# A hybrid decoder step on one core: the first stage's products put in the order in which their loads land, one gate tile's load issued ahead of a wait, and one block-diagonal product for the sample rows of a mixture window

## The reference, cut to what matters

```
mod = silu(c) @ w_ada + b_ada                      # six vectors per conditioning row: shift, scale, gate, twice
h = rms_norm(x, norm_mix_w) * (1 + sc1) + sh1
dn_qkv, dn_z, dn_a, dn_b, ssm_xbc, ssm_z, ssm_dt, gate_dn, gate_ssm = split(h @ w_in)
q, k, v = silu(causal_conv(dn_qkv, dn_conv_buf)); o, dn_state = gated_delta(q, k, v, g(dn_a), beta(dn_b))
x_, B, C = silu(causal_conv(ssm_xbc, ssm_conv_buf)); y, ssm_state = ssd(x_, dt(ssm_dt), B, C)
merged = sigmoid(gate_dn) * (o @ w_dn_out) + sigmoid(gate_ssm) * (y @ w_ssm_out)
x = x + gt1 * (merged @ w_out)
h = rms_norm(x, norm_ffn_w) * (1 + sc2) + sh2
x = x + gt2 * moe(h)                               # 4 groups x 8 experts, top-1 group, top-2 experts, SwiGLU, MOE_FF = 256
y = rms_norm(x, final_norm_w) * (1 + scale) + shift
```

## Time and profile before

| | |
|---|---|
| median of 3 executions | 838.47 us (837.27 to 840.47) |
| the profiled execution | 839.85 us |
| its span, first to last instruction | 838.1 us |
| mean granted TensorE clock | 0.942 |
| PE busy | 728.8 us, 87% of the span |
| chain that ended last: PE | 81% |
| DVE, ACT, POOL busy | 264.0, 195.1, 97.5 us |
| DMA | 195.88 MB, mean 234 GB/s |

### The profile page before, as it was taken

One profiled execution on the slowest core, in us unless ns is written; L12 is line 12 of the kernel. 1 busy time (PEld: TensorE's weight loads), 2 busy tenths in 40 slices (PEclk: granted clock), 3 DMA queues, 4 the chain that ended last, 5 costly groups with the idle time before them and its releaser, 6 DMA issues.

```text
span 838.1 us, 19950 instructions
## 1 busy us (share of the span) xinstructions
PE 728.8 (87%) x8393; PEld 529.4 (63%) x8394; DVE 264.0 (32%) x737; ACT 195.1 (23%) x500; POOL 97.5 (12%) x229
## 2 busy tenths in 40 slices
PE   2779999999988975998988999973998989999985
PEld 1567777787766654776766777733655656656554
DVE  0145412430134350666683112144111111111122
ACT  1221113112731322122223200051111112121225
POOL 7000000001011222100000000001212221222200
PEclk9869999999999996999998999985899999999996
DMA  7835579999444954651002706875899999999901
GB/s 264 228 103 201 201 245 327 327 327 334 121 112 122 260 148 103 200 179 26 1 2 74 266 0 268 334 300 204 313 413 411 414 413 411 415 412 414 385 15 56
DMA packets 108728, 195.88 MB, mean 234 GB/s; under 512 B 9964, under 2 KB 71097, under 8 KB 100488
## 3 DMA queue, kind: packets, MB, share of 16 engines
q1 hardware_dynamic: 106760, 189.94, 63.1%
q0 software_dynamic: 1920, 5.25, 1.7%
HBM read 185.40 MB, written 9.77 MB: 233 GB/s over the span
## 4 chain that ended last, share of the span: by engine, by line
PE 81%; DVE 6%; DMA 4%; issue 4%; ACT 3%; SPq 1%; POOL 0%; ACTq 0%; DVEq 0%; POOLq 0%
PE ps L1142 17%; PE ps L533 10%; PE ps L1212 7%; PE ps L506 5%; PE ps L546 5%; PE ps L430 4%; PE ps L451 4%; PE ps L1084 4%; PE ps L509 3%; PE ps L434 2%; PE ps L496 2%; DMA arena<-in_w_ada 1%; SPq L811 1%; PE ps L540 1%; DVE arena L1894 1%
## 5 line engine op out<-in xcount | busy, mean ns | idle before, releaser
L1142 PE MATMUL ps<-arena 128*128 128x288 f32 x576 | 144.8, 411 | 0.0
L1142 PEld LDWEIGHTS ps<-arena 128*128 128x128 f32 x576 | 109.3, 192 | 31.2 <-issue 1.0
L533 PE MATMUL ps<-arena 128*32 128x128 f32 x2432 | 86.7, 278 | 15.3 <-issue 12.8
L533 PEld LDWEIGHTS ps<-arena 128*32 128x32 f32 x2432 | 69.3, 111 | 39.4 <-issue 38.2
L1212 PE MATMUL ps<-arena 128*128 128x288 f32 x256 | 76.2, 427 | 14.2 <-DMA arena<-in_w_in 10.3
L1212 PEld LDWEIGHTS ps<-arena 128*128 128x128 f32 x256 | 45.3, 194 | 30.1 <-DMA arena<-in_w_in 10.6
L506 PE MATMUL ps<-level,arena 32*128 32x256 f32 x624 | 44.8, 401 | 0.5 <-DVE arena L775 0.5
L546 PE MATMUL ps<-arena,hact 128*32 128x256 f32 x608 | 40.7, 385 | 0.0
L770 DVE TENSOR_TENSOR h_row<-h_row,ps 128x64 f32<-128x64 f32 x38 | 8.4, 221 | 96.6 <-ACT h_row L628 96.6
L404 POOL DMA_INDIRECT arena<-h_rows,idx_now x38 | 37.6, 988 | 9.5 <-issue 9.5
L1084 PE MATMUL ps<-arena,cT 128*32 128x128 f32 x1024 | 33.8, 292 | 4.6 <-DMA arena<-in_w_ada 4.6
(11 more groups left out here) (432 smaller groups left out, 983.0 us busy)
## 6 DMA issues: line engine op xcount, KB each, us to landing
arena<-in_w_exp_gate SPq DMA_DIRECT2D x32, 1024.0 KB
arena<-in_w_exp_up SPq DMA_DIRECT2D x32, 1024.0 KB
arena<-in_w_exp_down SPq DMA_DIRECT2D x32, 1024.0 KB
arena<-in_w_ada SPq DMA_DIRECT2D x12, 2048.0 KB, 10.2
arena<-in_w_in SPq DMA_DIRECT2D x18, 1024.0 KB, 5.9
arena<-in_w_ada_final SPq DMA_DIRECT2D x4, 2048.0 KB, 14.9
arena<-in_w_in SPq DMA_DIRECT2D x16, 512.0 KB, 4.7
arena<-in_state_ssm_rec SPq DMA_DIRECT2D x8, 512.0 KB, 6.0
```

The source lines that it names most:

```text
L533: l = mm(ps[CW * q:CW * (q + 1), 5, 0:P].rearrange("p (g f) -> p g f", g=2), xwin[:, at:at + CW], gate_up[:, :, k, f:f + HF], start=(k == ...
L1142: l = mm(ps[:, 2 + 2 * sl + m, 0:TOK], w_ring[sl][:, k, m * P:(m + 1) * P], HN[:, k, :], start=(k == 0), stop=(k == KT - 1))
```

## The change

In the first stage PE's stream is rewritten: the w_ada tiles one and two no longer stand behind the tables; x's transposes, the tables' transposes, tile three, the sum of squares and tile four follow. `busy(n, bank)` multiplies the identity by itself n times into a bank that is not read. DVE makes HN's product with the inverse root ahead of the fourth w_ada tile's copy, and shares the scale and shift with ACT (four of eight row tiles each). The 24 small columns are made with `wsm` as the stationary operand (8 products of 288 columns, a result of 24 rows), in `project(0)` between its two w_in tiles with the first halo's transposes; `small_rows` turns them to token rows after the second. On SP the first two w_in tiles are issued ahead of the small loads, and gate 7's load behind the first half's four stores instead of behind the wait for them and gates 8 to 11.

In the windows, PT gets 384 columns: 256 for the prompt and 4 times 32 for the samples. `iota` is -1 in those of the 128 sample columns that don't belong to a partition's own group of 32, so that PT is block-diagonal there, and one product of 128 by 128 replaces the four of 32 by 32.

```diff
+        PTW = SEQ + 4 * SMP
+        PT, iota = late[:, 0:PTW], late[:, PTW:2 * PTW]
...
-            link(g.iota(iota, pattern=[[1, TOK]], base=0, channel_multiplier=0, allow_small_or_imprecise_dtypes=True))
+            link(g.iota(iota[:, 0:SEQ], pattern=[[1, SEQ]], base=0, channel_multiplier=0, allow_small_or_imprecise_dtypes=True))
+            own = iota[:, SEQ:PTW].rearrange("p (m t) -> p m t", t=SMP)
+            link(g.iota(own, pattern=[[0, 4], [1, SMP]], base=SEQ, channel_multiplier=0, allow_small_or_imprecise_dtypes=True))
+            for step, base in ((-SMP, 0), (SMP, SMP - 1)):
+                link(g.affine_select(out=own, in_=own, pattern=[[step, 4], [0, SMP]], base=base,
+                                     channel_multiplier=1 if step < 0 else -1, compare_op=ALU.is_ge, fill=-1.0))
...
-                for m in range(4):
-                    r = slice(CW * m, CW * (m + 1))
-                    l = mm(ps[r, 4, 0:2 * P], PT[r, SEQ:TOK], y_row[r, :], start=False, stop=last)
+                l = mm(ps[:, 4, 0:2 * P], PT[:, SEQ:PTW], y_row[:, :], start=False, stop=last)
...
-                ts(PT, iota[:, 0:TOK], slot_tab[:, 0, bass.ds(c, 1)], slot_tab[:, 1, bass.ds(c, 1)], ALU.is_equal,
+                ts(PT, iota, slot_tab[:, 0, bass.ds(c, 1)], slot_tab[:, 1, bass.ds(c, 1)], ALU.is_equal,
                    ALU.mult).then_inc(S("pt"), 1)
...
+            for sl in range(2):
+                load(w_ring[sl], wi[:, :, sl * WN:(sl + 1) * WN], f"win_ld{sl}")
             load(wsm[:, :, 0:4], wi[:, :, C_A:C_A + 4], "small_ld")
...
-            for sl in range(2):
-                load(w_ring[sl], wi[:, :, sl * WN:(sl + 1) * WN], f"win_ld{sl}")
...
+            e.wait_ge(S("gate_mm"), 5)
+            gate_load(6)
             for g in range(2):
-                e.wait_ge(S("gate_mm"), 5 + g)
-                gate_load(6 + g)
                 for j in range(4):
                     e.wait_ge(S("hs_new"), 4 * g + j + 1)
                     e.dma_start(hs_out[(4 * g + j) * P:(4 * g + j + 1) * P], Hs_g[g][:, j]).then_inc(S("hs_stored"), 16)
+                if g == 0:
+                    e.wait_ge(S("gate_mm"), 6)
+                    gate_load(7)
...
-            e.wait_ge(S("tab_ld"), 16 * 10)
-            tr(ps[:, 0, 0:A_ROWS], tabA, ident[0:A_ROWS, 0:A_ROWS])
-            tr(ps[:, 0, 128:128 + B_ROWS], tabB, ident[0:B_ROWS, 0:B_ROWS]).then_inc(S("first_mm"), 1)
-
...
+            def busy(n, bank):
+                for _ in range(n):
+                    mm(ps[:, bank, 0:P], ident[:, :], ident[:, :], start=True, stop=True)
             e.wait_ge(S("cT"), 1)
-            for i in range(2):
-                for sl in range(2):
-                    e.wait_ge(S(f"ada_ld{sl}"), i * 16 + 16)
-                    if i:
-                        e.wait_ge(S("mod_read"), sl + 1)
-                    ada_products(sl, 6 + sl)
-                    e.wait_ge(S("mod_row"), 2 * i + sl + 1)
-                    ada_transposed(sl, 6 + sl)
-                if i == 0:
-                    e.wait_ge(S("x_ld"), 48)
-                    for k in range(KT):
-                        if k >= 4:
-                            e.wait_ge(S("xT"), k - 3)
-                        for t, (o, p) in enumerate(TILES):
-                            l = tr(ps[:, k % 4 + 2, o:o + p], x_tok[0:p, t, k * P:(k + 1) * P], ident[0:p, 0:p])
-                        l.then_inc(S("x_mm"), 1)
+            busy(8, 0)
+            def first_block(i):
+                sl = i % 2
+                e.wait_ge(S(f"ada_ld{sl}"), i // 2 * 16 + 16)
+                if i >= 2:
+                    e.wait_ge(S("mod_read"), i - 1)
+                ada_products(sl, 6 + sl)
+                e.wait_ge(S("mod_row"), i + 1)
+                ada_transposed(sl, 6 + sl)
+            first_block(0)
+            busy(3, 0)
+            first_block(1)
+            busy(3, 0)
+            e.wait_ge(S("x_ld"), 48)
+            for k in range(KT):
+                if k >= 4:
+                    e.wait_ge(S("xT"), k - 3)
+                for t, (o, p) in enumerate(TILES):
+                    l = tr(ps[:, k % 4 + 2, o:o + p], x_tok[0:p, t, k * P:(k + 1) * P], ident[0:p, 0:p])
+                l.then_inc(S("x_mm"), 1)
+            e.wait_ge(S("tab_ld"), 16 * 10)
+            tr(ps[:, 1, 0:A_ROWS], tabA, ident[0:A_ROWS, 0:A_ROWS])
+            tr(ps[:, 1, 128:128 + B_ROWS], tabB, ident[0:B_ROWS, 0:B_ROWS]).then_inc(S("first_mm"), 1)
+            first_block(2)
             e.wait_ge(S("sq"), 1)
-            e.wait_ge(S("col"), 1)
             for k in range(KT):
                 l = mm(ps[:, 0, 0:TOK], ones[:, :], sq[:, k, :], start=(k == 0), stop=(k == KT - 1))
             l.then_inc(S("ms_mm"), 1)
-            e.wait_ge(S("small_ld"), 16 * 14)
-            e.wait_ge(S("xT"), 8)
-            for i, halo in enumerate((dn_halo, ssm_halo)):
+            first_block(3)
+            def small_products():
+                e.wait_ge(S("small_ld"), 16 * 14)
+                for k in range(KT):
+                    l = mm(ps[0:24, 0, 0:TOK], wsm[:, k, :], HN[:, k, :], start=(k == 0), stop=(k == KT - 1))
+                l.then_inc(S("gsm_mm"), 1)
                 for m in range(NQ):
-                    l = tr(ps[:, 2 + i, m * 24:(m + 1) * 24], halo[:, m * P:(m + 1) * P], ident[0:24, 0:24])
+                    l = tr(ps[:, 1, m * 24:(m + 1) * 24], dn_halo[:, m * P:(m + 1) * P], ident[0:24, 0:24])
                 l.then_inc(S("halo_mm"), 1)
 
+            def small_rows():
+                e.wait_ge(S("gsm_row"), 1)
+                for m in range(NQ):
+                    l = tr(ps[:, 0, m * 24:(m + 1) * 24], ssm_halo[:, m * P:(m + 1) * P], ident[0:24, 0:24])
+                l.then_inc(S("halo_mm"), 1)
+                e.wait_ge(S("halo_read"), 1)
+                for t, (o, p) in enumerate(TILES):
+                    l = four(t, ps[:, 1, t * 24:(t + 1) * 24], gsm_rows[:, o:o + p], ident[0:24, 0:24])
+                l.then_inc(S("gsm_mm"), 1)
+            e.wait_ge(S("root"), 1)
+            busy(10, 0)
             e.wait_ge(S("hn"), 1)
             e.wait_ge(S("x_mod"), KT)
-            for t, (o, p) in enumerate(TILES):
-                for k in range(KT):
-                    l = four(t, ps[:, 1, t * 24:(t + 1) * 24], HN[:, k, o:o + p], wsm[:, k, :], start=(k == 0), stop=(k == KT - 1))
-            l.then_inc(S("gsm_mm"), 1)
-            e.wait_ge(S("halo_read"), 2)
-            e.wait_ge(S("mod_read"), 4)
...
+                    if first:
+                        (small_rows if sl else small_products)()
...
-                for k in range(KT):
+                for k in range(KT // 2 if n == 1 else KT):
...
+                if i == 2:
+                    e.wait_ge(S("first_mm"), 2)
+                    v.tensor_copy(colB[:], ps[:, 1, 128:128 + B_ROWS])
+                    link(v.tensor_copy(colA[:], ps[:, 1, 0:A_ROWS]))
+                if i == 3:
+                    e.wait_ge(S("root"), 1)
+                    for k in range(KT):
+                        l = tt(HN[:, k, :], xT[:, k, :], rstd[:], ALU.mult)
+                    link(l)
...
-            e.wait_ge(S("root"), 1)
-            modulated(HN)
+            e.nop().then_inc(S("x_scaled"), KT)
+            for k in range(KT // 2, KT):
+                ts(HN[:, k, 0:SEQ], HN[:, k, 0:SEQ], scl[:, k, 0:1], modT[:, SHIFT1 + k, 0:1], ALU.mult, ALU.add).then_inc(S("x_mod"), 1)
             samples_modulated(HN, SHIFT1, 1)
             e.nop().then_inc(S("hn"), 1)
+            e.wait_ge(S("gsm_mm"), 1)
+            v.tensor_copy(gsm_rows, ps[0:24, 0, 0:TOK]).then_inc(S("gsm_row"), 1)
```

31 lines of the change are left out of this document (13 added, 18 removed).

## The result

The changed kernel takes 826.43 us, median of 4 executions (822.88 to 828.61), beside 837.88 for the kernel before: a ratio of 0.9852, 95% interval 0.9827 to 0.9877. That is 11.4 us less by the medians, 12.4 by the ratio, where 23 were forecast; 815 and the range up to 822 were too low. The profiled execution took 827.56 us, with a span of 825.8 at a mean granted clock of 0.950.

A forecast was written before the change was run, and what follows sets the result against it. PE, busy 87% of the span and holding 81% of the last chain, was taken as the bound. 839.85 - 14.4 - 12.8 + 2.7 + 0.9 = 816.2, given as 815 because the profiled execution is 1.4 above the median; range 806 to 822.

The forecast's parts named there:

- the last ten products: First stage: the last ten identity products need 2.2 us, free while PE waits for DVE and ACT to make HN.
- the rival of a fallen clock: First stage, chance 12%: low clock costs block 2 1.7 us more and the sum of squares up to 3.9; 821 us.
- the 14.4: First stage: reordered loads and PE work end `project(0)` at 61.7 instead of 76.1, 14.4 us less; bounds 8 and 16.
- small loads hidden: First stage: small loads land at 45.5, 2.3 us before `project(0)`'s first half ends at 47.8, so PE does not wait.
- Gate 7: Gate 7's load ordered earlier: most of PE's 10.32 us wait goes and the clock stays up, 12.8 us less; bounds 9 and 13.4.
- The 2.98 for the clock: Gate products b = 2 to 7, second half: without the idle time they take 4.82 us, not 7.80.
- the tile's lateness: Gate 7's tile lands 0.1 to 1.0 us after PE is ready for it; 0.5 was taken.
- The rival "the wait only moves": Gate 7, chance 6%: its tile or gate 8's lands late behind the stores; half the 12.8 us stays, 821.5 us.
- Windows: The block-diagonal sample product costs 0.07 us more in each of 38 windows and the last sum, +2.7 us in all.
- The rivals of -5.5 and +7.8: Window product: without overhead -5.5 us (chance 10%, 807 us); with a wholly exposed weight load +7.8, an upper bound without its own chance.
- POOL ahead of the loop: Ahead of the expert loop: one more iota and two selects delay y_row, +0.9 us; bounds 0 and 2.5.
- The prediction's own list: Trace signs of a right forecast (tile order, `project(0)`'s times, gate wait, clock, window stretch) and of a wrong one.

The follow-up runs named there:

- e6: The changed kernel with 13 identity products in place of 3 ahead of x's transposes; 827.30 us, ratio 0.9859 to the kernel before.
- e2: The kernel before with only gate 7's load moved ahead of the wait for the first half's stores; 829.27 us, ratio 0.9887.
- e3: The kernel before with only the window edit (block-diagonal sample product, wider PT, longer iota chain); 844.39 us, ratio 1.0066.
- e5: The changed kernel with y_row zeroed ahead of POOL's longer iota and select chain; 821.92 us, ratio 0.9795 to the kernel before.
- e9: The changed kernel with four 32-row sample products again, wide PT and long POOL chain kept; 824.10 us, ratio 0.9820 to the kernel before.
- e10: The changed kernel with gate 7's load ordered between the second and third of the first half's stores; 824.05 us, ratio 0.9822 to the kernel before.
- e13: The changed kernel with four sample products again, wide PT and long chain kept, y_row zeroed ahead of the chain; 821.28 us, ratio 0.9796 to the kernel before.
- e11: The changed kernel with 13 identity products ahead of x's transposes, y_row zeroed first and gate 7's load between the stores; 817.01 us, ratio 0.9748 to the kernel before.
- e4: The changed kernel without its window edit, first stage and gate 7 still changed; 818.20 us, ratio 0.9759 to the kernel before.

## Why the prediction was wrong

**The step that failed: the clock in the first stage.** The prediction costed x's transposes at 4.35, block 2 at 1.95 and the last ten products at 2.2, all at full clock, and gave the rival of a fallen clock 12%, with the argument that after x's transposes and 1.60 us of idle time 1.95 had been measured at 30.16. The argument looked at the wrong pause. The new order put the idle time ahead of x (2.88 us) and not behind it, and there the clock fell. By e6, where PE was busy in that pause and the clock stayed whole, it cost 2.5 us in the transposes and 1.1 in block 2, and 0.4 at `project(0)`'s start, since the last ten products, at half speed, outlast the wait for HN (from the sum of squares' start on it is 12.14 us in e6 and 12.55 in the changed kernel). `project(0)` starts 4.05 us earlier in e6, at 40.88 for a forecast of 40. The rival had the right mechanism, but priced block 2 and the sum of squares (which ran at full clock, 4.05) and not the transposes.

The argument from 30.16 was weak in itself, since it rested on one execution. In e2 and e3, whose first stage is that of the kernel before, the same block came after a shorter wait and ran at the low clock:

```profile
24.63 4.35 PE L1111 MATMUL ps<-ident,arena 128*128 128x128 f32 x24
...
30.23 3.64 PE L1087 MATMUL ps<-arena,cT 128*32 128x128 f32 x64 [1.25 <-DMA arena<-in_w_ada]
```

in e2, and in e3:

```profile
29.99 3.50 PE L1088 MATMUL ps<-arena,cT 128*32 128x128 f32 x64 [0.77 <-DMA arena<-in_w_ada]
```

In e2 the granted clock is 1.00 through the transposes, has fallen 0.5 us after their end and is 0.50 from 29.50 on.

The Trainium skill (TensorE: Matmul & The Clock Gate, Part 4: PE-mode transpose) was cited for the rule that transposes don't count as work for the clock. In e6 the full clock stayed through 4.41 us of transposes, with identity products ahead and block 2 behind; in the changed kernel 6.95 us of them did not bring it back, and it returned at 31.0. e2's row at 30.23 fits the page, at 30.16 and e6 don't bear it out, though in e6 other products stood on both sides. That 6.95 us of transposes did not raise the clock agrees with it but is weak evidence: in the kernel before, from 35.81 on, half the clock also stayed until about 41.6, mostly with ordinary products. The prediction held one trace against the page; the rival that the page favoured, 821, was nearer to the result than 815, but its price was put on other terms.

**The rest of the 14.4.** `project(0)` was over at 67.07 for 61.7, 5.4 late. In e6 it was over at 63.11: 4.0 is the clock, and 1.4 stays with the clock whole. Of this, block 2's tile came 0.9 later than forecast (used at 26.14 for 25.2), and the pieces from `project(0)`'s start on took 0.5 more. Another 1.4 went to the projection loop, since A was only 7.6 shorter; there PE waits 0.86 us for a w_in tile at 133.00:

```profile
120.54 12.28 SPq L816 DMA_DIRECT2D arena<-in_w_in  x2
...
133.00 3.18 PE L1170 MATMUL ps<-arena 128*128 128x288 f32 x12 [0.86 <-DMA arena<-in_w_in]
```

(the second row is cut off where the view ends). The profile of the kernel before doesn't have this wait. But PE's earlier arrival alone doesn't make it: e5, e9 and e10, with the same first stage, and the four kernels in which PE comes 4 us earlier still don't have it either. Its cause stays open. And before's own profile was late here: A was 231.4 in it and 230.2 in e2 and e3, which have the same first stage, so 1.2 us of the baseline were never there to gain in a median. x was used at 21.26 for a forecast 19.5; how much of the 1.4 comes from that no run separates. The parts behind were right: small loads hidden, 4.06 for the small products (3.9), 0.92 for the halos (0.8).

**Gate 7: right in mechanism, -11.9 for -12.8.** The 2.98 for the clock was there (4.89 for 7.80). The term mis-sized was the tile's lateness: 1.30 for 0.5. From its order at 299.55 to its use at 305.42 it takes 5.9 us, not 4.7. The 4.7 was called that of a tile "alone", but the earlier trace rows gives the median of sixteen loads. That the last store and the four tiles behind it on the queue slow it is likely but not shown; ordered between the stores it landed after 5.2 (e10). Nor is 1.30 its only value: in e2 and e6 it was 2.6 and 2.8. The rival "the wait only moves" did not come; e10 takes the wait away.

**Windows: right.** 0.07 a window was forecast, 0.08 measured (E, +3.1 for +2.7). The Trainium skill (TensorEngine Tiling (Array Packing), Key Properties) only says that a change of tiling mode drains TensorE. The prediction's own conclusion from it, that an equal number of changes makes the edit cost zero, does not fit the 0.63 and 0.57 of the traces. The rivals of -5.5 and +7.8 fall.

**POOL ahead of the loop: the term that was least right for its size.** +0.9 was forecast, with 2.5 as the bound if the clock falls. D is 14.9 us on average in the four kernels with the short chain ahead of y_row, and 17.6 in the eight with the long one: 2.7, just above that bound, of which 1.2 is the longer wait, and the rest mostly the ten products at the lower clock. Why the clock is low there is open: in e2, with the short chain and the wait of 0.86, they take 7.94 us at 0.51, and in e5 and e13, with no wait for y_row, 6.8 at 0.59. With y_row first it is 15.0 (e5, e11, e13). The whole window edit is then 3.1 + 2.7 = 5.8 by the traces, 5.5 in e3, and 7.8 between the changed kernel and e4, where 4.6 us of C, which no edit touches, lie between the two traces.

**Summed up.** The forecast was 23.6 in profiled terms, the traces show 12.3: 14.4 - 7.6 = 6.8 short in the first stage, 0.9 at gate 7, 2.0 more in D than the forecast 0.9, 2.9 in C, and 0.4 less than forecast in E, with 0.9 of gain between the stretches: 11.3. What stays open is C's 2.9, which varies from 111.5 to 116.7 over the kernels whatever was edited; it was put down to the clock by its rows, but not produced by any edit.

The prediction's own list: the third tile's order, the 1.3 us wait, the clock in b = 2 to 7 and L514's stretch came as written; `project(0)`'s two times did not, and of the signs of a wrong forecast none came, because the list looked for a low clock only in the sum of squares.
